# Two feed-forward barriers replaced by separate places, and memory attention laid between its projections

## The chip, the cores and the metric

The kernel runs on one core of a Trainium2 chip: TensorE (matrix products), VectorE, ScalarE and GpSimd (elementwise work), SyncE (issues DMAs), an on-chip memory of 128 partitions (SBUF) and the accumulators that TensorE writes (PSUM, eight banks of 128 x 512 float32). The metric is the device time of one execution in microseconds, median of the runs.

## The reference

One program computes two transformer-like blocks on 512 tokens of width 1024, all in float32. Only the parts that the change touches are shown.

```python
# first block: twice (layer 0 and 1), after a Mamba-2 and a Conformer mixer
u = rms_norm(x, norm_ffn[l]) @ f_up_w[l]          # 1024 -> 2 x 2816
a, g = split(causal_conv3(u, f_conv_w[l], f_conv_b[l]))
x = x + (silu(a) * g) @ f_down_w[l]               # 2816 -> 1024
# second block, after self attention, a state space model and w_out
x = layer_norm(ALPHA * x + ..., ln1)
m = layer_norm(mem, mem_ln)                       # 256 rows
k, v = split(m @ w_xkv)                           # 1024 -> 512 and 512
q = x @ w_xq                                      # 4 heads of 128
x = layer_norm(ALPHA * x + softmax(q k^T * X_SCALE) v @ w_xo, ln2)
x = layer_norm(ALPHA * x + moe_ffn(x), ln3)       # router, 64 experts, shared expert
```

## The kernel before

Activations lie transposed: features on the partitions, 512 tokens along the free side, a tensor of 1024 features being 8 blocks of 128 x 512. Each engine has one program in a fixed order; they meet through semaphores (`wait_ge`, `then_inc`).

**Rounded products.** Most projections take their precision from three products of rounded numbers (float32r): weight and activation are each split into a rounded part ("hi") and the remainder ("lo"), and TensorE does hi x hi, hi x lo and lo x hi per block of 128 (`proj_split`, L1246). ScalarE makes the hi parts (`split_half`, L1943; `split_x`, L1960), VectorE subtracts to get the lo parts (L2556, L2569). A few projections, among them memory keys, queries, values and output, use plain float32 products instead (`tile`, L1205); the profile counts two matmul instructions for each of these.

**Weights.** SyncE loads them into a ring of two slots (`wring`) in three DMAs each (L673). `slot()` waits until the tiles that used the slot before are done:

```python
if state["slots"] >= NSLOT:
    sp.wait_ge(tile_done, tiles.v - state["last"])
```

For the down projection `loop(4, 2, 2, body2)` sets `state["last"]` to 1, so the first down slot is issued when 43 of the 44 up tiles are done. The lo part is written over the slot; the hi parts lie in `whi` (at the end of the arena) for up weights and in `wdhi` (over `uT` and `sq`, which hold the up projection's input) for down weights.

**Feed-forward.** The up projection has 11 slots of 4 tiles (5 loop turns of 2 slots, and one more), 44 tiles of 8 blocks, a pair of tiles giving one block of the gated product: VectorE scales each tile out of PSUM (L2633), convolves it (L2635, L2637), ScalarE does Silu (L2162), VectorE multiplies (L2848) into `ffa`, 22 blocks. Then comes a barrier of all engines (`phase_end`: drain, count, wait for the three others), since `ffhi`, the rounded `ffa`, and the hi weights take memory that the up projection uses. After it `split_both` rounds the first half of the first down weights, 11 blocks, the second half, 11 blocks, and TensorE runs 8 down tiles of 22 blocks.

**Memory attention.** PE's order: key projection (4 tiles, 8 blocks, 256 columns), statistics of the layer norm, value projection (2 tiles), query projection (4 tiles), 16 items (4 heads by 4 groups of 128 tokens), output projection (8 tiles of 4 blocks). An item is: scores (TensorE, L1684), copy out of PSUM (VectorE, L3147), maximum (L3148), its negative (L3149), exponential with sum (ScalarE, L2341), reciprocal and product (VectorE, L3154, L3156), two transposes (TensorE, L1691), copy (ScalarE, L2349), product with the values (TensorE, L1699). PE works on scores of item n, transposes of n - 2 and values of n - 3 in one step. VectorE copies each head's result (L3160, L3162). Key, query and output weights are used as they were loaded.

**After it** come residual, layer norm, router, shared expert and then 64 experts, whose weights are loaded by L926 and L933; the first of these loads waits for the root of the last norm (`sp.wait_ge(std_ready, NORMS)`).

Of the kernel before, what the change touches and what calls it, by code (L numbers as in the profile page):

```python
# [32 lines left out]
P = 128  # L33
T = 512
# [115 lines left out]
def build(nc, A, out):  # L150

    ctx = ExitStack()
    with ctx:
# [163 lines left out]
        sgate = [carve(T) for _ in range(2)]  # L317
        ffhi = carve_r(FFN_TILES, T)
        ffhi_end = top[0]
# [74 lines left out]
        top[0] = NBANK * T + (2 * FFN_TILES + 2) * T  # L394
        assert top[0] >= ffhi_end
# [3 lines left out]
        bim = carve(S5T, 16)  # L399
        el = carve(STEPS, S5T)  # L400
        phs = carve(STEPS, S5T)
        phc = carve(STEPS, S5T)
        phr = std[:, 0:STEPS * S5T].rearrange("p (m j) -> p m j", j=S5T)
# [45 lines left out]
        memc = carve(NK, 256)  # L449
        top[0] = GATE_TOP  # L450
        memq = carve(NK, 256)
# [8 lines left out]
        vx = carve(2, T)  # L460
        top[0] = NBANK * T
        ox = carve(4, T)
# [189 lines left out]

        def phase_end(eng, me, ph):

            ph.inc()
            eng.drain().then_inc(done[me], 1)
            for other in done:
                if other != me:
                    eng.wait_ge(done[other], ph.v)


        @block.sync
        def _(sp):
# [232 lines left out]
            for e in done:  # L896
                sp.wait_ge(done[e], 6)
# [82 lines left out]
            with sp.If(crowded > CAP):  # L980
                for e in done:
                    sp.wait_ge(done[e], 7)
# [4 lines left out]
                for e in done:  # L987
                    sp.wait_ge(done[e], 8)
# [31 lines left out]
        def _(pool):  # L1020
# [22 lines left out]
            for _ in range(4):  # L1043
                phase_end(pool, "pool", ph)
# [134 lines left out]
        def _(pe):  # L1179
# [252 lines left out]
            def ffn():  # L1432
# [11 lines left out]
                phase_end(pe, "pe", ph)  # L1444

                with pe.Fori(0, 2) as i:
                    tiles.enter(i, 4)
                    slots.enter(i, 4)
                    nw.enter(i, 8)
                    for q in range(4):  # L1450
                        proj_split(FFN_TILES, ffhi, ff_lo, wdhi, range(1), fresh=q == 0)
                tiles.leave(2)
                slots.leave(2)
                nw.leave(2)
                nx.inc(FFN_TILES)

            ffn()
# [37 lines left out]
            ffn()  # L1495
# [180 lines left out]
            def attention(s, n_items, per_head, blocks, q, k, v, o, probs, turned, before):  # L1676

                for n in range(n_items + 3):
                    if n < n_items:
                        before(n)  # L1680
                        if n >= 2:
                            pe.wait_ge(s["masked"], n - 1)
                        nb = blocks(n)
                        nc.tensor.matmul(mp[n % 2][:, 0:nb * P], q(n), k(n, nb), start=True, stop=True).then_inc(s["scores"], 1)  # L1684
                    m = n - 2
                    if 0 <= m < n_items:
# [3 lines left out]
                        for j in range(blocks(m)):  # L1690
                            ins = nc.tensor.transpose(mp[2][:, j * P:(j + 1) * P], probs[m % 3][:, j * P:(j + 1) * P], ident[:])  # L1691
                        ins.then_inc(s["turned"], 1)
                    m = n - 3
                    if 0 <= m < n_items:
                        pe.wait_ge(s["evac"], m + 1)
                        if m % per_head == 0 and m:
                            pe.wait_ge(s["out"], m // per_head)
                        for j in range(blocks(m)):
                            ins = nc.tensor.matmul(o(m), v(m, j), turned[m % 2][:, j * P:(j + 1) * P],  # L1699
                                                   start=j == 0, stop=j == blocks(m) - 1)  # L1700
                        ins.then_inc(s["pv"], 1)

# [30 lines left out]
            w = slot_wait()[:, :].rearrange("p (k n) -> p k n", n=512)  # L1733
            for m in range(4):
                tile([(w[:, k, m * P:(m + 1) * P], mT[:, k, :]) for k in range(NK)], n=256)
# [7 lines left out]
            proj(NK, hT, 4)  # L1743
            q_tiles = tiles.s - 4

            def query_taken(n):
                if n % TC == 0:
                    pe.wait_ge(tile_evac, q_tiles + n // TC + 1)

            attention(att[1], 16, 4, lambda n: 2,  # L1750
                      lambda n: qx[:, n // TC, (n % TC) * P:(n % TC + 1) * P],
                      lambda n, nb: kx[:, n // TC, :],
                      lambda n, j: vx[:, j, (n // TC) * P:(n // TC + 1) * P],
                      lambda n: mp[3][:, (n % TC) * P:(n % TC + 1) * P],
                      xpb, xpt, query_taken)
            pe.wait_ge(att[1]["out"], 4)
            proj(4, ox, 8)
# [155 lines left out]
        def _(act):  # L1913
# [240 lines left out]
            def ffn(each=None):  # L2154
# [11 lines left out]
                with act.Fori(0, 5) as i:  # L2166
# [5 lines left out]
                tiles.leave(5), nconv.leave(5), nsilu.leave(5), nglu.leave(5), slots.leave(5)  # L2172
# [12 lines left out]
            ffn()  # L2185
# [51 lines left out]
            ffn(state_exponentials)  # L2237
# [98 lines left out]
            def attention(s, n_items, blocks, scale, probs, turned, nmx, rsm, after):  # L2336
# [1233 lines left out]
```

## Time and profile before

| | us |
|---|---|
| median of 3 runs (lowest, highest) | 2917.62 (2913.74, 2921.96) |
| the profiled execution | 2924.28 |
| its span, first to last instruction | 2922.5 |
| busy: TensorE / VectorE / ScalarE / GpSimd | 2710.5 / 1989.0 / 1381.3 / 230.7 |
| mean granted TensorE clock | 0.967 of full |

The span is what the profile covers; the execution's own time lies 1.8 us above it. A busy TensorE includes queued instructions: the duration of a matmul (about 0.4 us) is longer than the distance between two. So a rate is read from the length of an unbroken stretch of the chain divided by its matmuls.

### The profile page before, as it was taken

The page shows a single profiled execution, that of the slowest core. Times are in us where ns is not written, and L with a number is a line of the kernel's source. Part 1 is how long each engine was busy: PE and PEld are TensorE (multiplying, and loading weights), DVE is VectorE, ACT ScalarE, POOL GpSimd, SP SyncE. Part 2 cuts the span into 40 slices and gives each one's busy share as a digit, 9 for nine tenths or more (in the row PEclk, how much of TensorE's full clock was granted, in tenths as well). Part 3 has the DMA queues.
Part 4 walks back from the last instruction along what each step waited for, and adds up shares of the span by engine and source line. Part 5 has one row for each costly group of instructions (what it writes and reads, how often), then busy time and mean ns, then how long its engine had stood idle before and what let it go on. Part 6 is the DMA issues. An engine that isn't in the chain of part 4 may idle for free.

```text
span 2922.5 us, 36040 instructions
## 1 busy us (share of the span) xinstructions
PE 2710.5 (93%) x12225; PEld 2050.5 (70%) x12225; DVE 1989.0 (68%) x3048; ACT 1381.3 (47%) x2121; POOL 230.7 (8%) x207
## 2 busy tenths in 40 slices
PE   7999899999897989999899988999799999999996
PEld 6777778788786867888776755675357777777773
DVE  4677645677626975777538555454549999999986
ACT  4666543222324545222324333433338777777772
POOL 0000000000000000000004400000012222222210
PEclk9999999999999999999999998999899999999998
DMA  3222312232232101231633550323149999999996
GB/s 104 65 65 58 93 60 87 87 104 97 60 99 86 58 29 58 87 112 60 103 97 117 135 104 17 126 83 112 59 164 363 342 339 345 348 338 343 338 348 266
DMA packets 317001, 435.00 MB, mean 149 GB/s; under 512 B 45275, under 2 KB 198947, under 8 KB 316643
## 3 DMA queue, kind: packets, MB, share of 16 engines
q1 hardware_dynamic: 299139, 395.61, 41.8%
q0 software_dynamic: 17760, 38.06, 4.3%
q8 instruction: 60, 0.98, 0.1%
q14 instruction: 42, 0.34, 0.0%
HBM read 416.33 MB, written 42.43 MB: 157 GB/s over the span
## 4 chain that ended last, share of the span: by engine, by line
PE 64%; SPq 19%; DVE 8%; ACT 4%; issue 3%; DMA 2%; DVEq 0%; ACTq 0%; POOLq 0%
PE tp L1246 42%; SPq L926 12%; SPq L933 7%; PE tp L1205 5%; PE tp L1299 2%; PE tp L1301 2%; PE tp L1300 2%; DMA sq<-ytab 1%; PE mp L1474 1%; PE mp L1473 1%; PE mp L1475 1%; PE mp L1666 1%; PE mp L1265 1%; PE mp L1646 1%; DMA uT<-in_w_exp_gu 1%
## 5 line engine op out<-in xcount | busy, mean ns | idle before, releaser
L1246 PE MATMUL tp<-sq_r,arena_r 128*128 128x512 f32 x1152 | 464.3, 403 | 38.6 <-DVE uT_r L2569 25.7
L1246 PE MATMUL tp<-sq_r,wring_r 128*128 128x512 f32 x1152 | 459.4, 399 | 0.0
L1246 PE MATMUL tp<-uT_r,arena_r 128*128 128x512 f32 x1152 | 457.0, 397 | 0.0
L1246 PEld LDWEIGHTS tp<-sq_r,arena_r 128*128 128x128 f32 x1152 | 218.3, 190 | 98.8 <-issue 45.0
L1246 PEld LDWEIGHTS tp<-uT_r,arena_r 128*128 128x128 f32 x1152 | 218.7, 190 | 54.2 <-issue 1.9
L1246 PEld LDWEIGHTS tp<-sq_r,wring_r 128*128 128x128 f32 x1152 | 218.4, 190 | 53.6
L1246 PE MATMUL tp<-arena_r,wring_r 128*128 128x512 f32 x608 | 241.6, 397 | 0.0
L2556 DVE TENSOR_TENSOR wring_r<-wring,arena_r 128x2048 fp32r<-128x2048 f32 x80 | 182.5, 2322 | 61.8 <-ACT arena_r L1943 61.8
L2162 ACT ACTIVATE arena<-arena 128x512 f32<-128x512 f32 x44 | 27.8, 632 | 292.6 <-DVE arena L2637 292.5
L1943 ACT ACTIVATE arena_r<-wring 128x2048 fp32r<-128x2048 f32 x80 | 148.6, 1905 | 34.1 <-DMA wring<-in_a_out_proj 10.9
L1246 PE MATMUL tp<-arena_r,uT_r 128*128 128x512 f32 x480 | 152.7, 400 | 7.7 <-DVE arena_r L2569 7.7
L1246 PE MATMUL tp<-arena_r,sq_r 128*128 128x512 f32 x480 | 152.2, 398 | 7.7 <-DVE arena_r L2569 7.7
L1930 ACT ACTIVATE raw<-tp 128x512 f32<-128x512 f32 x74 | 43.7, 598 | 233.5 <-PE tp L1246 175.8
L3422 DVE TENSOR_TENSOR arena_r<-arena,arena_r 128x1024 fp32r<-128x1024 f32 x128 | 150.4, 1216 | 0.5 <-ACT arena_r L2470 0.5
L2637 DVE SCALAR_TENSOR_TENSOR arena<-raw,pcol,arena 128x512 f32<-128x512 f32 x176 | 132.3, 752 | 24.4 <-DVE arena L2637 6.1
L1299 PE MATMUL tp<-sq_r,wring_r 128*128 128x512 f32 x320 | 133.8, 418 | 8.7 <-issue 8.7
L1246 PEld LDWEIGHTS tp<-arena_r,wring_r 128*128 128x128 f32 x608 | 115.5, 190 | 27.1
L1301 PE MATMUL tp<-sq_r,wring_r 128*128 128x512 f32 x320 | 129.5, 405 | 0.0
L1300 PE MATMUL tp<-uT_r,wring_r 128*128 128x512 f32 x320 | 129.4, 405 | 0.0
L2470 ACT ACTIVATE arena_r<-arena 128x1024 fp32r<-128x1024 f32 x128 | 127.8, 1050 | 0.0
L1138 POOL DMA_INDIRECT ytab<-arena x64 | 90.2, 1409 | 467.4 <-ACT arena L2487 467.4
L2633 DVE TENSOR_TENSOR raw<-tp,rinv 128x512 f32<-128x512 f32 x88 | 60.5, 687 | 83.6 <-PE tp L1246 83.3
(531 smaller groups left out, 5923.6 us busy)
## 6 DMA issues: line engine op xcount, KB each, us to landing
arena<-in_w_exp_down SPq DMA_DIRECT2D x64, 1024.0 KB, 17.8
wring<-in_w_exp_gu SPq DMA_DIRECT2D x64, 768.0 KB, 9.8
uT<-in_w_exp_gu SPq DMA_DIRECT2D x32, 768.0 KB, 9.9
sq<-in_w_exp_gu SPq DMA_DIRECT2D x32, 768.0 KB, 10.4
wring<-in_f_up_w SPq DMA_DIRECT2D x22, 1024.0 KB, 5.2
wring<-in_f_up_w SPq DMA_DIRECT2D x44, 512.0 KB, 6.7
wring<-in_w_exp_gu SPq DMA_DIRECT2D x32, 512.0 KB, 16.8
wring<-in_f_down_w SPq DMA_DIRECT2D x32, 448.0 KB, 5.8
```

The costliest lines, as they stand in the source:

```text
L926: sp.dma_start(dst[:, a:z, :], gu[:, a:z, :]).then_inc(wg_ready[b], 16)
L933: sp.dma_start(wdn[b].rearrange("p (k n) -> p k n", n=D), dn).then_inc(wd_ready[b], 16)
L1205: ins = nc.tensor.matmul(b[lo:hi, 0:n], w, x, start=k == 0, stop=k == len(mms) - 1)
L1246: ins = nc.tensor.matmul(b[:], parts[wp][:, kk, m * P:(m + 1) * P], xparts[xp][:, kk, :], start=n_k == 0 and q == 0, stop=n_k == k - 1 and ...
L1299: nc.tensor.matmul(bank[:], w_hi[:, kk, cs], u_hi[1][:, kk, :], start=kk == 0, stop=False)
L1300: nc.tensor.matmul(bank[:], w_hi[:, kk, cs], u_lo[1][:, kk, :], start=False, stop=False)
L1301: ins = nc.tensor.matmul(bank[:], w_lo[:, kk, cs], u_hi[1][:, kk, :], start=False, stop=kk == NK - 1)
L1943: nc.scalar.activation(hi[r][1][:, a:b], wring[r][:, a:b], ACT.Copy).then_inc(whi_ready, 1)
L2470: nc.scalar.activation(wdn_hi[b][:, s], wdn[q][:, s], ACT.Copy).then_inc(moe["dhi"], 1)
L2556: V.tensor_tensor(wlo[r][:, a:b], wring[r][:, a:b], hi[r][1][:, a:b].bitcast(F32), ALU.subtract).then_inc(wlo_ready, 1)
L2637: ins = V.scalar_tensor_tensor(dst, r[:, PAD - t:PAD - t + T], w(taps - 1 - t), dst, ALU.mult, ALU.add)
L3422: V.tensor_tensor(wdn_lo[q][:, s], wdn[q][:, s], wdn_hi[b][:, s].bitcast(F32), ALU.subtract).then_inc(moe["dlo"], 1)
```

## The change

- `ffhi` moves to the end of the arena, the hi part of the first down slot's "early" weights gets a place of its own (`first_whi`). `FFN_EARLY` names the blocks whose place is free before the up projection ends: 0 to 13 in layer 0, 0 to 5 and 14 to 18 in layer 1; the others are "late".
- The barrier goes. ScalarE and VectorE round the first 9 early blocks between the last pairs of the up projection, then the first slot's early weights, the other early blocks, the last pair, the late weights and the late blocks. TensorE runs the first down tile in that order of blocks (`first_down`), and the down loop is written out.
- GpSimd takes part in two barriers instead of four; its loads for the state space model follow the Conformer's barriers. Waits on the barrier counts are renumbered.
- The key projection becomes a rounded one (`key_hi`, `mT_hi`, `mT_lo`), the output projection too (`ox_hi`, `ox_lo`).
- Query tiles 2 and 3 and 12 of the 32 blocks of the output projection stand between the steps of the attention. The maximum and the exponential read the scores from PSUM, without the copy. Heads 0 and 2 are summed in banks of the ring of tiles.

```diff
@@ places
+        FFN_EARLY = (list(range(14)), list(range(6)) + list(range(14, 19)))
+        FFN_LATE = [[k for k in range(FFN_TILES) if k not in ks] for ks in FFN_EARLY]
+        first_whi = carve_r(max(len(ks) for ks in FFN_EARLY), P)
+        top[0] = ARENA - FFN_TILES * T
         ffhi = carve_r(FFN_TILES, T)
...
+        key_hi = [None, carve_r(SLOT)]
+        ox_hi = carve_r(4, T)[1]
@@ TensorE
+            def first_down(layer):
+                early = len(FFN_EARLY[layer])
...
+                for n_k, kk in enumerate(FFN_EARLY[layer] + FFN_LATE[layer]):
+                    if n_k in (0, early):
+                        pe.wait_ge(wlo_ready, nw.v + 1)
+                        nw.inc()
+                    pe.wait_ge(xlo_ready, nx.s + n_k + 1)
+                    high = first_whi[1][:, n_k, :] if n_k < early else whole[:, kk, :]
+                    nc.tensor.matmul(b[:], high, ffhi[1][:, kk, :], start=n_k == 0, stop=False)
+                    nc.tensor.matmul(b[:], high, ff_lo[1][:, kk, :], start=False, stop=False)
+                    ins = nc.tensor.matmul(b[:], low[:, kk, :], ffhi[1][:, kk, :], start=False, stop=n_k == FFN_TILES - 1)
...
-                phase_end(pe, "pe", ph)
-                with pe.Fori(0, 2) as i:
...
+                first_down(layer)
+                for m in range(1, NK):
+                    proj_split(FFN_TILES, ffhi, ff_lo, wdhi, range(1))
...
+            QUERY_STEPS = [(0, 1), (2, 3), (4, 5), (6, 7), (0, 1), (2, 3), (4,), (5,), (6, 7)]
+            OUT_STEPS = {9: ((0, 0),), 10: ((1, 0),), 11: ((2, 0),), 12: ((0, 1),), 13: ((1, 1),), 14: ((2, 1),), 15: ((0, 2),),
+                         16: ((1, 2), (2, 2)), 17: ((3, 0), (3, 1)), 18: ((3, 2),)}
+            def memory_attention(n_weights, n_rows):
+                for n in range(16 + 3):
+                    if n < 16:
...
+                        if n >= 2:
+                            pe.wait_ge(s["exped"], n - 1)
+                        nc.tensor.matmul(mp[n % 2][:, 0:256], qx[:, h, c * P:(c + 1) * P], kx[:, h, :], start=True, stop=True)
...
+                    if n < 9:
+                        query_piece(2 + n // 4 if n < 7 else 3, QUERY_STEPS[n])
+                    for m, k in OUT_STEPS.get(n, ()):
+                        out_piece(m, k, n_weights, n_rows)
@@ ScalarE
-                for p in range(2):
-                    pair(p)
-                phase_end(act, "act", ph)
-                split_both(wdhi, FFN_TILES, P, ff_lo, ffhi)
+                pair(0)
+                split_weight(whi, NK, 512)
+                down_hi(early[0:2])
+                pair(1)
+                down_hi(early[2:4])
+                pair(2)
+                split_weight(whi, NK, 512)
+                down_hi(early[4:6])
+                pair(3)
+                act.wait_ge(tile_done, first_tile + 40)
+                down_hi(early[6:9])
+                pair(0)
+                r = slot_in()
+                first_weights(r, early, lambda a, b: first_whi[1][...])
+                down_hi(early[9:])
+                pair(1)
+                act.wait_ge(tile_done, first_tile + 44)
+                first_weights(r, late, lambda a, b: wdhi[r][1][:, a * P:b * P])
+                down_hi(late)
...
+            take(qx[:, 0, :])
+            split_weight(wdhi, 4, 1024)
+            take(qx[:, 1, :])
...
+                if n in (4, 9):
+                    take(qx[:, 2 + n // 9, :])
+                if n in (7, 11, 15):
+                    take_heads(n // 4 - 1)
@@ VectorE
-                phase_end(dve, "dve", ph)
-                split_both(wdhi, FFN_TILES, P, ff_lo, ffhi)
+                pair(16, 0)
+                split_weight(whi, NK, 512)
+                split_x(ff_lo, ffhi, early[0:2])
+                pair(17, 1)
+                split_x(ff_lo, ffhi, early[2:4])
+                pair(18, 2)
+                split_weight(whi, NK, 512)
+                split_x(ff_lo, ffhi, early[4:6])
+                pair(19, 3)
+                split_x(ff_lo, ffhi, early[6:9])
+                pair(20, 0)
+                first_weights(r, early, lambda a, b: first_whi[1][...])
+                split_x(ff_lo, ffhi, early[9:])
+                pair(21, 1)
+                first_weights(r, late, lambda a, b: wdhi[r][1][:, a * P:b * P])
+                split_x(ff_lo, ffhi, late)
...
-                            link(V.tensor_copy(p[:, 0:nb * P], bank[:, 0:nb * P]))
-                        link(V.tensor_reduce(mx[:, n:n + 1], p[:, 0:nb * P], AX.X, ALU.max))
+                    link(V.tensor_reduce(xsm[0][:, n:n + 1], mp[n % 2][:, 0:256], AX.X, ALU.max))
...
+                if n in (7, 11, 15):
+                    low_heads(n // 4 - 1)
```

## Rows read from the trace of the kernel before

**Rows 1.** The page's part 4: the chain that ended last, shares by engine.
```profile
PE 64%; SPq 19%; DVE 8%; ACT 4%; issue 3%; DMA 2%; DVEq 0%; ACTq 0%; POOLq 0%
```

**Rows 2.** Windows, us: busy by engine (instructions), granted clock, DMA share, GB/s.
```profile
2400.00:2600.00 200.00, 187.99 (x930) 145.66 (x931) 182.68 (x282) 151.06 (x224) 43.78 (x38) 0.99 0.99 344
```

**Rows 3.** Waits of SyncE's queue from 2100 us on: total, times, longest.
```profile
SPq L926 <- ACT std L1987: 13.0, 1, 13.0
```

**Rows 4.** The whole chain in order of time: start us, us, what.
```profile
517.93 246.41 PE tp L1246 x1056
...
772.03 124.80 PE tp L1246 x528
...
1405.25 125.55 PE tp L1246 x528
```

**Rows 5.** The same chain, 755 to 800 us, piece by piece.
```profile
764.37 0.70 DVE raw L2633
...
767.32 0.69 DVE arena L2848
...
768.15 1.39 ACT sq_r L1943
...
769.66 1.62 DVE wring_r L2556
```

**Rows 6.** Windows of 1 us around the start of the down projection.
```profile
769.00:770.00 1.00, 0.00 (x0) 0.00 (x0) 0.34 (x1) 1.00 (x3) 0.00 (x0) 0.62 1.21 289
...
776.00:777.00 1.00, 1.00 (x6) 0.82 (x5) 1.00 (x3) 1.00 (x3) 0.00 (x0) 0.97 0.00 0
```

**Rows 7.** Windows: key projection, query projection, memory attention, output projection.
```profile
1971.94:1985.75 13.81, 13.81 (x66) 12.16 (x65) 9.66 (x15) 5.89 (x11) 0.00 (x0) 1.00 0.37 133
2001.04:2028.69 27.65, 27.65 (x66) 12.34 (x65) 0.00 (x0) 2.39 (x4) 0.00 (x0) 1.00 0.28 88
2028.69:2066.62 37.93, 26.55 (x128) 19.41 (x127) 24.83 (x84) 16.01 (x50) 0.00 (x0) 0.82 0.17 56
2066.62:2094.40 27.78, 27.78 (x65) 12.46 (x66) 9.00 (x13) 4.18 (x7) 0.00 (x0) 1.00 0.00 0
```

**Rows 8.** Timeline of SyncE's queue, 755 to 775 us.
```profile
758.89 7.84 SPq L673 DMA_DIRECT2D wring<-in_f_down_w  x6
```

**Rows 9.** Instructions on the weight slots, 755 to 775 us: landing.
```profile
DMA to landing us min/median/max: 4.1/5.1/5.9
```

**Rows 10.** Timelines of ScalarE and VectorE: start, us, line, operation, count.
```profile
729.05 3.71 ACT L1943 ACTIVATE arena_r<-wring 128x2048 fp32r<-128x2048 f32 x2
...
734.78 4.49 DVE L2556 TENSOR_TENSOR wring_r<-wring,arena_r 128x2048 fp32r<-128x2048 f32 x2
...
769.43 5.82 ACT L1960 ACTIVATE arena_r<-arena 128x512 fp32r<-128x512 f32 x11
...
771.20 6.70 DVE L2569 TENSOR_TENSOR arena_r<-arena,arena_r 128x512 fp32r<-128x512 f32 x11
```

**Rows 11.** Timeline of TensorE's weight loads in the expert stage.
```profile
2302.78 0.53 PEld L1796 LDWEIGHTS mp<-arena_r 128*128 128x128 f32 x4
```

**Rows 12.** Timeline of VectorE during w_out; in brackets the idle time before.
```profile
1964.50 0.69 DVE L2652 SCALAR_TENSOR_TENSOR hT<-hT,raw 128x512 f32<-128x512 f32 x1 [4.16 <-ACT raw L1930]
```

**Rows 13.** The chain inside the memory attention, 2028 to 2067 us.
```profile
2032.82 0.60 ACT arena L2341 x2
...
2049.19 0.45 PE mp L1699 x4
2049.63 0.45 PE mp L1684 x2
...
2050.56 0.43 DVE arena L3148
...
2062.69 0.22 PE mp L1691 x2
```

**Rows 14.** DMA issues, 2001 to 2003 us: line, KB each, us to landing.
```profile
wring<-in_w_xo SPq DMA_DIRECT2D x1, 1024.0 KB, 8.4
```

More of the change, by code:

```diff
@@ L651, in build, with runs @@
         s5_yev = ssd["ea"]
+        def runs(ks):
+            starts = [k for k in ks if k - 1 not in ks]
+            return [(a, next(b for b in range(a + 1, FFN_TILES + 1) if b not in ks)) for a in starts]
         def phase_end(eng, me, ph):
@@ L987, in _ @@
                 for e in done:
[L988 removed]
+                    sp.wait_ge(done[e], 6)
                 load_rest()
@@ L1674, in mixed_heads, with query_piece @@
                         chunk_results(*Y_AT[n])
[L1676 to L1680, printed above, removed]
+            def query_piece(m, ks):
+                if ks[0] == 0:
+                    pe.wait_ge(tile_evac, QUERY_TILE + m - NBANK + 1)
+                w = wring[1][:, :].rearrange("p (k n) -> p k n", n=512)
+                for k in ks:
+                    ins = nc.tensor.matmul(tp[(QUERY_TILE + m) % NBANK][:], w[:, k, m * P:(m + 1) * P], hT[:, k, :],
+                                           start=k == 0, stop=k == NK - 1)
+                if ks[-1] == NK - 1:
+                    ins.then_inc(tile_done, 1)
@@ L1742, in _ @@
             pe.wait_ge(h_ready, 3 * NK)
[L1743 to L1757, printed above, removed]
+            slot_wait()
+            assert tiles.s == QUERY_TILE
+            for m in range(2):
+                query_piece(m, range(NK))
+            slots.inc()
+            memory_attention(nw.v, nx.v)
+            for m in range(4):
+                out_piece(m, 3, nw.v, nx.v)
+            for m in range(4, 8):
+                for k in range(4):
+                    out_piece(m, k, nw.v, nx.v)
+            tiles.inc(12)
+            nw.inc(2)
+            nx.inc(4)
             sum_rows(hT, 2, OUT_CONVS)
@@ L2152, in _, with ffn, down_hi, first_weights @@
             root(0, D, 0)
-            def ffn(each=None):
+            def ffn(layer, each=None):
+                products, first_tile = 2 + nglu.s, tiles.s
+                early, late = FFN_EARLY[layer], FFN_LATE[layer]
+                def down_hi(ks):
+                    for kk in ks:
+                        act.wait_ge(glu_ready, products + kk + 1)
+                        split_x(ff_lo, ffhi, (kk,))
+                def first_weights(r, ks, spot):
+                    for a, b in runs(ks):
+                        ins = nc.scalar.activation(spot(a, b), wring[r][:, a * P:b * P], ACT.Copy)
+                    ins.then_inc(whi_ready, 1)
                 def pair(p):
@@ L2848, in pair, with first_weights @@
                     V.tensor_tensor(at(ffa, p), sgate[b % 2][:], acc[(2 * b + 1) % NBANK][:], ALU.mult).then_inc(glu_ready, 1)
-                with dve.Fori(0, 5) as i:
+                early, late = FFN_EARLY[layer], FFN_LATE[layer]
+                def first_weights(r, ks, spot):
+                    dve.wait_ge(whi_ready, nw.v + 1)
+                    for a, b in runs(ks):
+                        ins = V.tensor_tensor(wlo[r][:, a * P:b * P], wring[r][:, a * P:b * P], spot(a, b).bitcast(F32), ALU.subtract)
+                    ins.then_inc(wlo_ready, 1)
+                    nw.inc()
+                with dve.Fori(0, 4) as i:
                     tiles.enter(i, 8), nconv.enter(i, 8), nsilu.enter(i, 4), chain.enter(i, 16), nglu.enter(i, 4)
```

216 lines of the change are left out of this document (126 added, 90 removed).

## The prediction

> **What bounds the kernel now.** I read the profile in this order. First the chain that ended last, by engine [rows 1]: TensorE holds 64% of it and the weight DMAs of the experts another 19%. So up to about 2190 us a gap on TensorE is time, and after that the DMA of expert weights is. Two rows [rows 2, 3] say how the two join: the DMA engines are 99% busy between 2400 and 2600, and SyncE's loads for the experts wait for a norm root that ends the TensorE part. What TensorE saves earlier therefore starts the expert stage earlier by the same amount and is not given back.
>
> Then the places where the chain leaves TensorE. In the first feed-forward the up projection ends at 764.34 (517.93 + 246.41) and the down projection starts at 772.03 [rows 4]: 7.7 us of nothing. The chain inside it [rows 5] is strictly serial: the last up tile is read and convolved (764.37 to 767.3), gated (0.69), then the barrier opens, ScalarE rounds half the first weights (1.39), VectorE takes the remainder (1.62) and one activation block, and TensorE begins. The granted clock falls to half inside the gap and is full again only about 4 us after the restart [rows 6]. By the up projection's 246.41 / 1056 = 0.2333 us a matmul, 528 down matmuls need 123.2; they took 124.8 and 125.55 in the two layers [rows 4], so the clock costs another 1.6 and 2.3. Each barrier costs 9.3 to 10 us today, both together 19.3.
>
> The memory attention is the other hole [rows 7]: query projection 27.65, attention 37.93 with TensorE busy 26.55 of it (queued instructions and low clock included, granted clock 0.82), output projection 27.78. Sum 93.36.
>
> **Feed-forward barriers: what comes instead.** The barrier goes, but the load of the first down weights is not touched: SyncE issues it at 758.89, when tile 43 of 44 is done, 5.5 us before the up projection ends [rows 8], and a part takes up to 5.9 us to land [rows 9]. The third part is issued about 0.6 us after the first and more, so the slot is full at about 765.4, 1.0 after TensorE runs dry. Before, the barrier covered that. Now it is first in the new chain, and what is queued behind it matters: VectorE has "first weights" in its program ahead of the last pair (tiles 42 and 43), so it stands still from about 757 and does not read tiles 42 and 43 until the weights are through. ScalarE has the last pair's Silu behind its own copy too.
>
> Layer 0, in order. Rounding 14 blocks, 1792 columns, at 3.71 / 4096 us a column [rows 10]: 1.65, to 767.05. Remainder on VectorE at 4.49 / 4096: 2.0, to 769.1. TensorE restarts at 769.25, 2.8 earlier than now, still after a gap of 4.9 us in which I expect the clock to fall. VectorE goes on with 5 activation blocks at 0.61 (6.70 / 11, [rows 10]) to 772.15; the last pair, 2 x 2.86 (764.37 to 767.32, less hops) + 0.69 + hops = 6.5 [rows 5], to 778.65; the late 8 weight blocks 1.15, to 779.8; the first late activation block 0.61, so TensorE's late part begins at 780.6. TensorE has 14 x 0.70 = 9.8 us of early blocks, done at 779.05 or, with half clock, about 781. Eight late blocks take 5.6: the first down tile ends at about 786.4. Now it ends at 772.03 + 15.4 + 1.6 = 789.0. Gain 2.6. The clock loss hides in the wait for the late part, so it costs almost nothing, and the earlier restart gains little.
>
> Layer 1 rounds 11 blocks early, in two pieces. Weights 1398.6, rounding 1.5, remainder 1.7, restart 1402.0; 2 activation blocks to 1403.1; last pair to 1409.6; 11 late weight blocks 1.7, first activation block, late part at 1412.05, 11 x 0.70 = 7.7, end 1419.75, against 1405.25 + 15.4 + 2.3 = 1422.95. Gain 3.2. Both layers: 5.8.
>
> At nothing I set: the activation blocks rounded during the up projection (9 per layer, 0.53 on ScalarE and 0.61 on VectorE each). They start behind pair 16; VectorE needs 2.86 x 2 + 0.69 = 6.4 us a pair against 11.2 us of TensorE, plus 4.5 for weights in every second one [rows 10]. The last up weights are then ready at about 738.7, while TensorE asks for them at 742; without that cover of 3 us each block would cost 0.61. Also at nothing: the second down tile's weights (VectorE free at 784.7, + 1.6 = 786.3, just in time; a slip costs at most about 1 us), GpSimd's small loads (now some 300 us earlier, where nothing waits), and the unrolled loops.
>
> Bounds for this part: 0 if the new chain is as long as the old one, 19.3 if the hole closes wholly.
>
> **Key projection.** 32 k-blocks of float32 with 256 columns (13.81 us, [rows 7]) become 96 rounded ones. No row has a rounded matmul of 256 columns. From one side half of the 512-column 0.2333 is 0.117; from the other, four 128-column weight loads with almost no data took 0.53, 0.13 each [rows 11]. I take 0.126: 12.1 us, a gain of 1.7. The far bound is 0.2333 as for 512 columns: 22.4 us, a loss of 8.6. The new roundings (8 blocks of 256 and a whole weight slot: some 7 us on ScalarE, 8 on VectorE) fall on w_out's tiles 3 to 6, where VectorE sits idle 4.2 us of each 5.6 [rows 12] and ScalarE has less to do than it, and so cost nothing; without that cover they would cost their 8 us.
> The Trainium skill, "TensorE: Matmul & The Clock Gate", section "LDWEIGHTS (loading the stationary operand)", gives columns / 1.2 in ns, 107 ns for 128 columns, whatever the rows. By that rule a rounded block would not be held by its weight load, 96 would take about 11.2 by half the 512-column figure, and this term would be 2.6; the row's 0.13 is above it, so I stay by the row.
>
> **Memory attention.** The output projection turns from 32 float32 blocks (27.78 / 32 = 0.87) into 32 of three rounded matmuls (3 x 0.2333 = 0.70): 22.4, 5.4 less. An item of attention costs TensorE, at full clock, scores 0.45, two transposes 0.22, values 0.45 [rows 13]: 1.12, 17.9 for 16. TensorE's work is then 27.65 + 17.9 + 22.4 = 67.95. Two query tiles go ahead (13.8); the other two (16 blocks) and 12 output blocks are laid between the items; 20 blocks follow (14.0). A step has 1.12 + 1.73 = 2.85 us up to step 8 and 1.82 after. The loop between the engines: score 0.45, maximum 0.43 straight from PSUM (the copy of 0.43 goes), sign 0.17, exponential 0.60, copy of the turned block 0.38, with hops 2.1 [rows 13]: it fits into 2.85 and just into 1.82 + 0.45. Waits that I find by following every step: the output weights are issued at 2001.24 and the last part lands 8.4 us later [rows 14], so rounding (3.7) and remainder (4.5) run until about 2017 and the first maximum is 1.8 late: 1.1 at the third item. Output block (0, 2) in step 15 needs head 2, which ScalarE and VectorE round only behind their own step 15: 0.43 + 0.17 + 0.60 + 0.38 + 0.60 + 0.70 and hops, less TensorE's 0.7: 2.5. Smaller ones of that kind (steps 12 and 13, and the last head): 2.1. Sum 5.7, total 73.6, gain 19.8. Bounds: no wait at all 25.4; a full extra microsecond in each of 19 steps, under 1.
>
> Sum: 5.8 + 1.7 + 19.8 = 27.3. The profiled execution took 2924.28 (span 2922.5), so it would be 2897; it lies 6.7 above the median of 2917.62, from which I forecast **2890.3**.
>
> **Rivals.** A, the hole closes wholly: a gain of 19.3 instead of 5.8, 2876.8. For it: the first gated blocks and VectorE's time are there. Against: [rows 8, 9]; nothing can be rounded before 765. Chance 0.06.
> B, the interleaved attention is held by hops and the heads' rounding more than I count, 0.4 to 0.9 us in each of 19 steps: gain 10 to 20 in all, 2898 to 2908. The step's slack is only 0.1 to 0.2 from step 9 on. Chance 0.12.
> C, slower: items don't overlap. One item end to end is 0.45 + 0.43 + 0.17 + 0.60 + 0.18 + 0.37 + 0.22 + 0.38 + 0.45 with nine hops, about 4. If TensorE's order makes each step wait for the item of the step, 19 x 4 = 76 + 13.8 + 14 = 104, 10.5 more than now; with the other two terms 3 us slower, and beyond the bound at 4.3 us a step, 2927. Decides from 3.9 us a step. Today a step takes 37.93 / 16 = 2.4. Chance 0.01.
> D, it does little: the rounded key projection costs its upper bound and B comes on top, within 9 us of now. Chance 0.03.
> My forecast, gain 20 to 34: 0.78 (its own range 2883 to 2898).
>
> **How the numbers follow.** 0.3% is 8.8 us, about what a measurement of this kernel can tell from no change. Faster: A, B and mine, 0.96; same 0.03; slower 0.01. The range has A at one end and most of B at the other: 2877 to 2903.
>
> **What would show it.** After: TensorE idle 4 to 5 us, not 7.7, between up and down, ended by the first weights' remainder; VectorE idle about 10 us before that; a second pause of 1 to 2 us some 10 us into the first down tile. From the first query matmul to the last output matmul 72 to 76 us, full clock throughout, longest wait about 2.5 us in step 15. Key projection 12 us. Wrong if the slot lands earlier or the first weights don't wait for it, if VectorE doesn't finish the last up weights by 742, or if a 256-column rounded matmul costs above 0.15.

## The result and the profile after

The changed kernel takes 2891.3 us (median of 4 runs, 2887.08 to 2899.33), the kernel before 2918.25 (4 runs, 2913.74 to 2921.96). The ratio is 0.9912, 95% interval 0.9886 to 0.9937. That is 27.0 us faster; the forecast was 2890.3, a gain of 27.3. The profiled execution took 2899.33 (span 2897.6, mean granted clock 0.973 where before had 0.967).

In after's lines, L1263 is the rounded projection (before L1246), L1463 to L1465 the first down tile, L1712 a query block, L1727 to L1729 an output block, L2243 (ScalarE) and L2975 (VectorE) the first down weights, L3432 the remainder of a head.

The chain by engine is within a point what it was [rows 1]: TensorE, then the experts' DMAs.

```profile
PE 64%; SPq 19%; DVE 7%; ACT 3%; issue 3%; DMA 2%; DVEq 0%; ACTq 0%
```

**The feed-forwards.** The chain of after in order of time, the lines that answer to [rows 4]:

```profile
518.97 246.40 PE tp L1263 x1056
765.37 5.65 issue
...
789.31 107.30 PE tp L1263 x462
1151.28 246.63 PE tp L1263 x1056
1397.91 5.25 issue
...
1421.16 107.30 PE tp L1263 x462
```

The up projection is undisturbed (246.40 for 246.41), so the roundings put between its last pairs cost nothing. The hole is shorter, not closed: 5.65 and 5.25 us in place of 7.7. To compare both kernels without the border between two tiles, take the time from the end of up to the end of all eight down tiles. After: 789.31 + 107.30 - 765.37 = 131.24 and 1421.16 + 107.30 - 1397.91 = 130.55. Before: 772.03 + 124.80 - 764.34 = 132.49 and 133.24 in the same way. Gain 1.25 + 2.69 = 3.9 us.

What holds the hole open, in the timelines of ScalarE and VectorE (start, us, operation; in brackets the idle time before and what ended it):

```profile
767.16 1.70 ACT L2243 ACTIVATE arena_r<-wring 128x1792 fp32r<-128x1792 f32 x1 [14.55 <-DMA wring<-in_f_down_w]
```

```profile
768.89 2.02 DVE L2975 TENSOR_TENSOR wring_r<-wring,arena_r 128x1792 fp32r<-128x1792 f32 x1 [11.04 <-ACT arena_r L2243]
...
773.84 0.68 DVE L2753 TENSOR_TENSOR raw<-tp,rinv 128x512 f32<-128x512 f32 x1
...
780.15 1.22 DVE L2975 TENSOR_TENSOR wring_r<-wring,sq_r 128x1024 fp32r<-128x1024 f32 x1
781.29 1.89 DVE L2689 TENSOR_TENSOR arena_r<-arena,arena_r 128x512 fp32r<-128x512 f32 x3
```

ScalarE stands 14.55 us and VectorE 11.04 for a transfer that lands 1.79 us after TensorE has run dry (767.16 against 765.37). Behind it on VectorE stands the last pair, which begins at 773.84 though its tiles have been there since 765.37. Windows of 1 us (busy by engine, then the granted clock) show the other cost:

```profile
770.00:771.00 1.00, 0.00 (x0) 0.02 (x1) 1.00 (x2) 1.00 (x3) 0.00 (x0) 0.64 1.19 302
...
774.00:775.00 1.00, 1.00 (x4) 0.71 (x4) 0.96 (x2) 0.00 (x0) 0.00 (x0) 0.50 0.00 0
...
777.00:778.00 1.00, 1.00 (x5) 0.78 (x5) 0.93 (x3) 1.00 (x2) 0.00 (x0) 0.95 0.00 0
```

TensorE restarts at 771.01 at half clock (1.2 of 2.4 GHz) and has the full one only at about 777.1, 6.1 us later; before, it had it some 4 us after the restart [rows 6]. By the windows the low clock lasted the same 6.8 us in both traces (769.2 to 776.1 before, 770.3 to 777.1 after); before, 2.8 us of it fell into the gap, where it costs nothing, and after only 0.7.

**Key projection and memory attention.** Windows of after: key projection, two query tiles, attention with the other two and 12 output blocks between its steps, 20 output blocks. They answer to [rows 7].

```profile
1965.30:1976.76 11.46, 11.46 (x98) 11.31 (x96) 9.66 (x15) 5.78 (x11) 0.00 (x0) 1.00 0.46 169
1992.21:2005.94 13.73, 13.73 (x34) 6.08 (x32) 2.65 (x2) 4.90 (x4) 0.00 (x0) 1.00 0.56 177
2005.94:2051.50 45.56, 42.40 (x198) 29.75 (x196) 20.38 (x69) 18.57 (x56) 0.00 (x0) 0.96 0.15 47
2051.50:2065.70 14.20, 14.20 (x61) 11.48 (x62) 8.82 (x13) 4.20 (x7) 0.00 (x0) 1.00 0.01 2
```

Key projection 13.81 to 11.46. From the first query matmul to the last output matmul 93.36 to 73.5 (13.73 + 45.56 + 14.20). TensorE is busy 93% of the middle window where before it was 70%. Its waits in the whole stretch (total, times, longest), and the longest of them:

```profile
PE tp L1727 <- DVE arena_r L3432: 3.1, 3, 2.1
```

```profile
2042.97 0.47 PE L1727 MATMUL tp<-arena_r,uT_r 128*128 128x512 f32 x1 [2.11 <-DVE arena_r L3432]
```

Sum of the parts: 3.9 + 2.35 + 19.9 = 26.1 us, the spans differ by 24.9 and the medians by 27.0. That these agree so well is partly luck: two long stretches outside the parts differ by some 4 us each, in opposite directions. From the end of the second down to the key projection the trace before took 441.1 us and after 436.8; from the last output matmul to the end they took 828.1 and 831.9. The first difference lies in the state space part (chain of before 1704.84 to 1843.15, of after 1702.49 to 1836.92: 138.3 and 134.4). It follows the execution and not the change: mem_only, with the feed-forwards of before, takes 134.6 there, and warm_gap, with those of the change, 136.8.

### The profile page after: what moved, and what is told of

Same layout as the page of the kernel before. It is cut to its first block, busy times and chain, and to the rows that moved or that the text cites. A ratio compares the mean times of both kernels' runs of the same rounds, so it can differ in the third digit from the quotient of the medians.

```text
span 2897.6 us, 35998 instructions
## 1 busy us (share of the span) xinstructions
PE 2689.7 (93%) x12289; PEld 2048.6 (71%) x12289; DVE 1994.0 (69%) x3046; ACT 1389.5 (48%) x2137; POOL 230.2 (8%) x207
## 4 chain that ended last, share of the span: by engine, by line
PE 64%; SPq 19%; DVE 7%; ACT 3%; issue 3%; DMA 2%; DVEq 0%; ACTq 0%
PE tp L1263 41%; SPq L943 12%; SPq L950 7%; PE tp L1222 4%; PE tp L1316 1%; PE tp L1317 1%; PE tp L1318 1%; PE tp L1712 1%; DMA sq<-ytab 1%; PE mp L1504 1%; PE mp L1503 1%; PE mp L1505 1%; PE mp L1282 1%; PE mp L1696 1%; PE mp L1676 1%
## 5 line engine op out<-in xcount | busy, mean ns | idle before, releaser
L1263 PE MATMUL tp<-sq_r,arena_r 128*128 128x512 f32 x1152 | 463.6, 402 | 38.7 <-DVE uT_r L2689 25.3
L1263 PE MATMUL tp<-sq_r,wring_r 128*128 128x512 f32 x1152 | 459.3, 399 | 0.0
L1263 PE MATMUL tp<-uT_r,arena_r 128*128 128x512 f32 x1152 | 457.9, 398 | 0.0
L1263 PEld LDWEIGHTS tp<-sq_r,arena_r 128*128 128x128 f32 x1152 | 218.5, 190 | 99.7 <-issue 45.1
L1263 PEld LDWEIGHTS tp<-uT_r,arena_r 128*128 128x128 f32 x1152 | 218.7, 190 | 54.5 <-issue 1.9
L1263 PEld LDWEIGHTS tp<-sq_r,wring_r 128*128 128x128 f32 x1152 | 218.4, 190 | 53.1
L1263 PE MATMUL tp<-arena_r,wring_r 128*128 128x512 f32 x564 | 222.7, 395 | 0.0
L1263 PE MATMUL tp<-arena_r,sq_r 128*128 128x512 f32 x436 | 136.9, 396 | 0.0
L1263 PE MATMUL tp<-arena_r,uT_r 128*128 128x512 f32 x436 | 136.8, 395 | 0.0
L1263 PEld LDWEIGHTS tp<-arena_r,wring_r 128*128 128x128 f32 x564 | 106.3, 188 | 25.2
## 6 DMA issues: line engine op xcount, KB each, us to landing
sq<-in_w_exp_gu SPq DMA_DIRECT2D x32, 768.0 KB, 10.3
```

Of the source, the lines that this page charges most:

```text
L1263: ins = nc.tensor.matmul(b[:], parts[wp][:, kk, m * P:(m + 1) * P], xparts[xp][:, kk, :], start=n_k == 0 and q == 0, stop=n_k == k - 1 and ...
```

## Experiments

All times "query to output" below are from the first query matmul to the end of the last output matmul. "Down" is the time from the end of up to the end of the eight down tiles, both layers added: 265.7 before, 261.8 after. Seven versions ran once: heads_early 2887.62, warm_gap 2895.21, no_interleave 2897.55, copy_back 2899.23, copy_back_plain 2897.38, one_bank 2902.18, copy_one_plain 2907.36. Such a time can't tell a few microseconds (the kernel before took 2910.58 to 2928.17 in 13 runs, and copy_back_plain comes out below no_interleave, though its stretch is 4.75 us longer), so their verdicts rest on a stretch of the trace.

### ffn_only: the feed-forward part alone

The kernel before with the feed-forward hunks of the change (`first_down`, `FFN_EARLY`, `first_whi`, no barrier); key projection and memory attention as before.

> The kernel before with the feed-forward part of the change alone (own places for the rounded rows and for the first down weights). Theory, from the two traces: the first down tile ends 23.9 us after the up projection in layer 0 and 23.3 us in layer 1, where before it took 25.2 and 25.9, so the whole is 3.9 us faster than before (ratio 0.9987), all of it in these two gaps. Rival: the gain of the whole change was made elsewhere and the gaps give 0 or over 10 us.

Measured: 2913.99 (12 runs) against 2918.16 (17 runs), ratio 0.9983, interval 0.9972 to 0.9994, so 5.0 us, between 1.8 and 8.2. The chain:

```profile
762.39 5.61 issue
...
785.77 107.30 PE tp L1256 x462
...
1391.36 4.91 issue
...
1413.96 106.79 PE tp L1256 x462
```

Down is 130.68 + 129.39 = 260.1. The theory holds: the part is small and lies in the two gaps.

### mem_only: key projection and memory attention alone

The kernel before with the rest of the change; the barriers of the feed-forwards stay.

> The kernel before with the memory attention and the rounded key projection alone. Theory: key projection 11.5 us where before took 13.8, query start to last output matmul 73.5 us where before took 93.4: 22.2 us faster than before (ratio 0.9924). Rival: some of the gain seen in the attention stage needs the feed-forward part, and the ratio is above 0.994.

Measured: 2895.23 (4 runs), ratio 0.992, interval 0.9902 to 0.9939: 23.3 us. Query to output 73.5 (1993.92 to 2067.38), key projection 11.31, so 11.31 / 96 = 0.118 us for a rounded matmul of 256 columns:

```profile
1967.32 11.31 PE tp L1212 x96
```

The theory holds: this part needs nothing of the other, and 5.0 + 23.3 = 28.3 is the whole (25.7 by its ratio) within the intervals.

### early_load: the first down weights issued three tiles sooner

```diff
-                def body2(i):
-                    for j in range(2):
-                        slot(1, thirds(down, FFN_TILES, (2 * i + j) * P, P))
-                loop(4, 2, 2, body2)
+                for m in range(NK):
+                    slot(1, thirds(down, FFN_TILES, m * P, P))
```

> The changed kernel with the slots of the down projection written out, so that the first of them waits for 40 finished tiles of up where the loop makes it wait for 43. Theory (what holds the hole open is the late transfer of the first down weights): it is issued some 16 us earlier, the early roundings are done before the up projection ends, the engine never stops long enough to lose its clock, and the first down tile ends some 15.5 us after the up projection in both layers (66 products of 0.233 us): 16 us faster than the change, about 2875 us. Rival (the chain of the last pair on VectorE binds): the tile ends 20 us or more after it and the gain stays under 7 us.

Measured: 2872.65 (4 runs, 2870.94 to 2873.78), ratio to before 0.9845, interval 0.9827 to 0.9864. The change stands at 0.9912 (0.9886 to 0.9937), so this is some 18.6 us faster than it, of which 261.8 - 244.6 = 17.2 lie in the two gaps. The chain:

```profile
516.25 244.06 PE tp L1261 x1056
...
775.58 107.30 PE tp L1261 x462
1138.83 244.30 PE tp L1261 x1056
...
1398.40 106.79 PE tp L1261 x462
```

The first down tile ends 775.58 - 760.31 = 15.27 us after the up projection, and 15.27 in layer 1: 66 matmuls at 0.2314, no gap and no clock lost. Timelines of SyncE, ScalarE and VectorE, one fence each:

```profile
738.15 24.02 SPq L690 DMA_DIRECT2D wring<-in_f_down_w  x6
```

```profile
747.79 1.69 ACT L2241 ACTIVATE arena_r<-wring 128x1792 fp32r<-128x1792 f32 x1
```

```profile
752.82 2.02 DVE L2973 TENSOR_TENSOR wring_r<-wring,arena_r 128x1792 fp32r<-128x1792 f32 x1
...
765.22 4.91 DVE L2687 TENSOR_TENSOR arena_r<-arena,arena_r 128x512 fp32r<-128x512 f32 x8
```

The transfer is issued at 738.15, 22 us before up ends, where the change issues it 5.5 us before. The early weights are rounded at 752.82 to 754.84, inside the up projection, VectorE reads the last pair as soon as it is there, and the late blocks begin at 765.22, 4.9 us after up, where the change has them 15.9 after. The late transfer was the cause of the hole; the rival is refuted.

### early_load_before: the same edit to the kernel before

> The kernel before with the slots of the down projection written out in the same way. Theory: before, the barrier and the roundings behind it hold TensorE, and the weights have landed by then, or nearly; so the earlier transfer gives under 1 us for each layer (ratio 0.9993 to 1.000). Rival: the late transfer is a hold of its own before too, and gives 3 us or more for each layer.

Measured: 2918.09 against 2919.03, ratio 0.999, interval 0.9974 to 1.0007. The load goes out at 740.25 instead of 758.89, up ends at 762.63, down starts at 770.32, and the chain between them has the same roundings as in [rows 5]:

```profile
766.44 1.38 ACT sq_r L1941
...
767.95 1.63 DVE wring_r L2554
```

Down is 133.15 + 132.52 = 265.7, as before to 0.1 us. So the early load is worth nothing that can be measured with the barrier, and 16 to 17 us without it (244.6 against the 260.8 that eight profiles below have on average). The barrier hid the late transfer; taking the barrier away and leaving the transfer gave a fifth to a quarter of what the two give together.

### warm_gap: useless matmuls ahead of the first down tile

```diff
+                for _ in range(6):
+                    nc.tensor.matmul(mp[3][:], ones[:], hT[:, 0, :], start=True, stop=True)
                 first_down(layer)
```

> The changed kernel with six matmuls of no use ahead of the first down tile in each layer, on operands that are there already and into a bank that is free, so that TensorE is busy in the first half of the wait for the weights. Theory (the half clock after the hole costs time of its own): the clock falls later or not at all, and the first down tile of layer 0 ends 22.3 us after the up projection, where the change took 23.9; of layer 1 0 to 0.9 us sooner. Rival: the late roundings bind, and both stay within 0.3 us of 23.9 and 23.3.

Measured: first down tile 24.04 us after up in layer 0 and 24.6 in layer 1; neither theory nor rival, though layer 0 has the rival's number and layer 1 its mechanism, a wait for the late roundings. Down is 262.7, not less than the change's 261.8. In layer 1 TensorE keeps the full clock at the restart, and then this (TensorE's timeline, and its windows with the granted clock behind the busy share):

```profile
1392.80 5.31 PE L1484 MATMUL mp<-hT,ones 128*128 128x512 f32 x12
1398.17 0.47 PE L1463 MATMUL tp<-arena_r 128*128 128x512 f32 x1
...
1407.94 0.47 PE L1463 MATMUL tp<-arena_r,uT_r 128*128 128x512 f32 x1 [1.89 <-DVE arena_r L2691]
```

```profile
1399.00:1400.00 1.00, 1.00 (x6) 1.00 0.40 94
...
1411.00:1412.00 1.00, 1.00 (x3) 0.50 0.00 0
```

The early blocks are through at about 1405.8, the late ones are not rounded before 1407.9, 15.1 us after up ended, and the clock falls after that pause, where nothing covers it. In the change the late blocks began 15.4 us after up (1413.35 - 1397.91), so there were 0.3 us to gain here. In layer 0 the restart came 6.94 us after up where the change had 5.65, since the weights landed at 765.84, 3.09 us after up (1.5 to 2.0 in the eight other profiles with this part of the change; one run can't say why). From that restart the tile took 17.1 us, in the change 18.3: the clock was at half for 3.4 us of it (771.0 to 774.4 by the windows) where in the change it was for 6.1. So in layer 0 the shorter half clock gave 1.2 us of the tile; the hole itself stays.

### heads_early: the heads of the attention rounded one step sooner

```diff
-                if n in (7, 11, 15):
-                    take_heads(n // 4 - 1)
+                if n in (6, 10, 14):
+                    take_heads((n - 6) // 4)
...
-                if n in (7, 11, 15):
-                    low_heads(n // 4 - 1)
+                if n in (6, 10, 14):
+                    low_heads((n - 6) // 4)
```

> The changed kernel with the heads taken one step earlier, alone. Theory: the heads' rounding on VectorE is the wait (2.1 us at the last step, 0.7 and 0.3 us at two others); one step of 2.2 us earlier it falls to under 0.3 us in all, the clock does not fall, and the stretch from the first query matmul to the last output matmul takes some 70 us where the change takes 73.5. Rival: the waits stay, since what the rounding waits for is no sooner done.

Measured: query to output 71.2 (1985.55 to 2056.76), full clock in all of it. TensorE's waits in the stretch:

```profile
PE mp L1755 <- ACT arena L2533: 1.4, 3, 0.6
PE tp L1727 <- DVE arena_r L3432: 1.1, 2, 0.7
```

The 2.1 us wait and the clock loss are gone; 1.4 us of new, short waits on the transposes came: in the chain a head's rounding on ScalarE (0.50) and its remainder on VectorE (0.69) now stand ahead of the next item's maximum. 2.3 us of the expected 3.5.

### both: early load and earlier heads

> The early first down weights together with the heads of the memory attention taken one step earlier (steps 6, 10 and 14 where the change has 7, 11 and 15). Theory: 16 us from the holes and some 3.5 us from the waits at the ends of the steps (2.1 us before the third item of the last steps, with the clock lost behind it), so 19 us faster than the change, about 2872 us. Rival: the heads' exponentials and copies are late for an earlier step, the waits move and give nothing, about 2875 us.

Measured: 2871.69 (4 runs, 2868.36 to 2874.59), ratio to before 0.9844, interval 0.9825 to 0.9863. It is the fastest of all, but 1.0 us from early_load is less than these runs can tell; in the trace, query to output is 71.2 in it and 73.4 in early_load. The forecast of 19 us below the change came out at 19.6.

### no_interleave: nothing between the attention's steps

```diff
-                    if n < 9:
-                        query_piece(2 + n // 4 if n < 7 else 3, QUERY_STEPS[n])
-                    for m, k in OUT_STEPS.get(n, ()):
-                        out_piece(m, k, n_weights, n_rows)
...
-            for m in range(2):
+            for m in range(4):
                 query_piece(m, range(NK))
```

and all 32 output blocks behind the attention.

> The changed kernel with all four query tiles ahead of the memory attention and all output pieces behind it, nothing between the attention's steps, with the roundings as in the change. Theory: the fillers take up waits of the attention chain, so without them the stretch from the first query matmul to the last output matmul takes some 83 us where the change takes 73.5 (before: 93.4, with full-precision instructions of the plain kind in the projections). Rival: the gain lies in the rounded projections alone, and it stays within 76 us.

Measured: 77.7, between the two. Query projection, attention, output projection:

```profile
1987.64:2015.30 27.66, 27.66 (x66) 12.35 (x65) 4.49 (x2) 6.79 (x6) 0.00 (x0) 1.00 0.28 88
2015.30:2042.95 27.65, 20.07 (x129) 15.10 (x128) 17.65 (x67) 15.94 (x53) 0.00 (x0) 1.00 0.24 77
2042.95:2065.35 22.40, 22.40 (x98) 18.18 (x98) 9.70 (x14) 4.79 (x8) 0.00 (x0) 1.00 0.00 1
```

I had missed that the steps themselves got shorter: 27.65 for the same 16 items that took 37.93 before [rows 7], at full clock where before had 0.82. The fillers are worth only 4.2 us. The next four ask where the other 10.3 come from.

### copy_back, copy_back_plain: the copy of the scores put back

In the changed kernel, and in no_interleave:

```diff
+                    if n >= 3:
+                        dve.wait_ge(s["turned"], n - 2)
+                    link(V.tensor_copy(xpb[n % 3], mp[n % 2][:, 0:256]))
-                    link(V.tensor_reduce(xsm[0][:, n:n + 1], mp[n % 2][:, 0:256], AX.X, ALU.max))
+                    link(V.tensor_reduce(xsm[0][:, n:n + 1], xpb[n % 3], AX.X, ALU.max))
...
-                    nc.scalar.activation(xpb[n % 3], mp[n % 2][:, 0:256], ACT.Exp, scale=X_SCALE, ...
+                    nc.scalar.activation(xpb[n % 3], xpb[n % 3], ACT.Exp, scale=X_SCALE, ...
```

> The changed kernel with VectorE's copy of the scores out of PSUM put back: copy, maximum of the copy, exponential in place. Theory: the loop of an item grows by the copy (0.4 us) to 2.5 us; it still fits into the steps 0 to 8 with a query block (2.85 us) and costs 0.2 to 0.4 us in each of the ten later steps, so the stretch from the first query matmul to the last output matmul takes 75.5 to 77.5 us where the change takes 73.5. Rival: the later steps cover it too, and it stays within 0.5 us of 73.5.

Measured: query to output 76.6, 3.1 us more; the theory's size holds. Its place is shown in part: TensorE's listed waits grew by 1.3 us only (transposes 1.1, scores 0.2), and the clock loss is the change's; the other 1.8 us are in no list.

> The version with nothing between the attention's steps (27.7 us for the 16 items, 7.6 us of them waits, full clock) with the copy of the scores put back. Theory: without fillers the loop sets the step, each of 16 items gets 0.4 us longer, 6.4 us in all, and the 16 items take 34 us; the longer waits also take some of the clock. Rival: less than half of it, under 31 us, since two items are under way at once.

Measured: query to output 82.5, 4.75 us more than no_interleave, 0.30 an item where the theory had 0.4, at full clock. The items take 32.4, short of the theory's 34 and over the rival's 31, and the clock loss that the theory also had did not come:

```profile
2013.80:2046.20 32.40, 21.10 (x129) 14.89 (x128) 23.89 (x83) 16.58 (x53) 0.00 (x0) 1.00 0.20 66
```

### one_bank, copy_one_plain: all heads in one accumulator

```diff
-        memory_out = [tp[QUERY_TILE % NBANK], mp[3], tp[(QUERY_TILE + 3) % NBANK], mp[3]]
+        memory_out = [mp[3]] * 4
...
-                        if c == 0 and h == 3:
-                            pe.wait_ge(xlo_ready, n_rows + 2)
+                        if c == 0 and h >= 1:
+                            pe.wait_ge(xlo_ready, n_rows + h)
```

In the changed kernel, and in copy_back_plain.

> The changed kernel with all four heads summed in the same PSUM bank, so that the first product with values of a head waits until ScalarE and VectorE have rounded the head before (in the change only head 3 waits, for head 1). Theory: two more waits of 1.5 to 2 us each, at steps 7 and 11, and some clock: the stretch from the first query matmul to the last output matmul takes 76.5 to 78.5 us where the change takes 73.5. Rival: a wait here only takes the place of the one at the output blocks (step 12 and 15), and it stays under 75 us.

Measured: query to output 80.5, 7.0 us more, above the theory's range and far from the rival. The waits of the stretch:

```profile
PE mp L1766 <- DVE arena_r L3432: 8.0, 3, 2.7
...
PE tp L1727 <- DVE arena_r L3432: 0.7, 1, 0.7
```

8.7 us of waits where the change has 3.1; the other 1.4 go with the clock (0.93 in the attention's window where the change has 0.96).

> Nothing between the attention's steps, the copy put back and one bank for all heads: the attention of the kernel before, rebuilt in the changed kernel, with the rounding of a head in the place of its copy. Theory: these two are the whole of the difference between 27.7 us (no fillers) and 37.9 us (before), so the 16 items take 37 to 41 us and the granted clock in them is below 0.9. Rival: something else in the change made up the difference, and they take under 34 us.

Measured: query to output 89.45; the 16 items 38.6 us at a clock of 0.89:

```profile
2016.30:2054.90 38.60, 24.56 (x129) 18.03 (x129) 24.17 (x83) 16.57 (x53) 0.00 (x0) 0.89 0.17 55
```

The attention of the kernel before is rebuilt, within 0.7 us of its 37.93. So the chain of versions accounts for the 19.9 us: 93.4 before; 89.45 with the output projection rounded (5.4 less, 0.7 more for the items, 0.8 of half clock behind them); 82.5 with heads in separate banks (7.0); 77.7 without the copy (4.75); 73.5 with the fillers (4.2). The price of an edit depends on its neighbours: the copy costs 3.1 with the fillers and 4.75 without.

## Why the prediction was right

- **Forecast 2890.3, measured 2891.3.** The terms 5.8, 1.7 and 19.8 came out as 3.9 (5.0 in ffn_only's timing), 2.35 and 19.9. What TensorE saves does start the experts' loads sooner: the first goes out at 2080.1 us where before had 2108.8, and 24.9 of these 28.7 us are left at the end of the span. That forecast and median lie 1.0 us apart is luck all the same: the interval of the ratio leaves a gain between 18.4 and 33.3 us.
- **The hole: shortened, not closed.** "First weights" waited for the transfer and VectorE stood still about 11 us, as forecast; TensorE's gap was 5.65 and 5.25 us where the forecast had 4 to 5. Rival A (19.3 us) did not come, for the reason given [rows 8, 9], and early_load shows that this reason is the only one: with the transfer out of the way down falls by 265.7 - 244.6 = 21.1, more than A's 19.3.
- **The term that was mis-sized: 5.8 us for both layers.** The pair of traces gives 3.9. Eight profiles of kernels with this part of the change as it stands (after, ffn_only, heads_early, no_interleave, copy_back, copy_back_plain, one_bank, copy_one_plain) have down between 259.9 and 261.8, mean 260.8; three without it (before, mem_only, early_load_before) 265.7, 266.7, 265.7, mean 266.0. That is 5.2, so of the 1.9 us that the pair of traces lacks 1.3 are variation between executions. Within the pair, two steps came out longer. The slot landed 1.8 and 2.0 us after up, not 1.0, and TensorE restarted 0.7 and 0.8 us later than forecast. And the step "The clock loss hides in the wait for the late part" failed: in layer 0 the half clock lasted 6.1 us after the restart where I had counted on the 4 us of before, the early part (done at 783.8) was then later than the first late block (ready at 781.9), nothing was left to hide in, and the tile took 18.3 us from the restart where I had 17.15 (layer 1: 18.0 for 17.75). Against that I had the first tile of before 1.1 us too short for both layers together (24.66 and 25.39 after up, against 25.19 and 25.94). My 786.4 is also a slip: 780.6 and eight blocks of 0.70 give 786.2. The second pause that I expected inside the first tile is absent since TensorE never caught up with VectorE; warm_gap, where TensorE kept the full clock through the early part of layer 1, brought it back there (1.89 us).
- **The key projection**: 0.118 us a matmul. I had taken 0.126, between 0.117 and 0.13. The rule of the Trainium skill ("TensorE: Matmul & The Clock Gate", section "LDWEIGHTS (loading the stationary operand)", 107 ns for 128 columns), by which the weight load would not hold a matmul of this size, was nearer than my row [rows 11]: it gave 2.6, the chain has 13.81 - 11.31 = 2.5.
- **The attention**: 73.6 forecast, 73.5 measured, but two errors cancel. I counted 5.7 us of waits, there were 3.1: none at the third item (the first maximum was 1.3 us late where I had 1.8, and its exponential was through at 2008.9, before TensorE came to the third scores at 2010.24), 2.1 of the 2.5 in step 15, 1.0 of the 2.1 small ones. Against that the clock, which I had at full throughout, fell behind the wait in step 15 (about 1.7 us lost by the windows below), and 0.7 us more are in no list of waits: 73.5 - 67.95 - 3.1 - 1.7. One_bank and copy_back cost 7.0 and 3.1 us, together about half of the gain. The prediction names the missing copy in its count of a step. The separate banks it does not name: that no head but one waits for the rounding of another is in its count unsaid, so it had the right sum without the part that was worth most.

## What to carry to other kernels

When a barrier is taken away, ask what it was covering: here a weight transfer that a loop's coarse wait (43 tiles where 40 are enough) let out too late. Neither edit alone was worth more than about 5 us of 2918, both together 21. And a useful cross-check of a forecast is to rebuild the old version inside the new one, one edit at a time: the interleaving, which looks like the point of the change, gave 4.2 of 19.9 us, while an accumulator bank of its own for every other head gave 7.0 (each price holds for this order of edits).

## What the runs showed that I had not expected

- **The clock falls in a busy stretch.** After the 2.11 us wait of step 15, TensorE's windows (busy, granted clock):

```profile
2042.00:2043.00 1.00, 0.03 (x1) 1.00 0.00 0
...
2044.00:2045.00 1.00, 1.00 (x6) 0.50 0.00 0
...
2047.00:2048.00 1.00, 1.00 (x10) 1.00 0.00 0
```

  About 3.4 us at half clock (0.72 in the window from 2043, 0.57 in that from 2046), with TensorE at work on both sides. In warm_gap the clock fell behind a wait of 1.89 us in the same way. Not every wait of this length does it: in copy_back_plain two of 1.80 us, and in one_bank the third of three waits of 2.67, left the clock at full; behind the two others of one_bank it fell. No run here says what decides.
- **How long the half clock lasts differs between executions of the same code**: in the first feed-forward it ran until 6.1 us after the restart in after and only until about 2.8 in no_interleave (769.57 to 772.4; the window from 772 has 0.82, the next 1.00). Counted from its fall, the low clock lasted 6.8 us in the one and 3.4 in the other, and 10.2 in the second feed-forward of before (1400.7 to 1410.9), behind the same 7.7 us gap as in the first, where it was 6.8. The first down tile ended 18.3 and 16.9 us after the restart accordingly.

```profile
772.00:773.00 1.00, 1.00 (x5) 0.79 (x4) 1.00 (x2) 0.00 (x0) 0.00 (x0) 0.82 0.00 0
```

  The second feed-forward of before (busy, granted clock):

```profile
1400.00:1401.00 1.00, 0.00 (x0) 0.85 1.13 341
...
1410.00:1411.00 1.00, 1.00 (x4) 0.53 0.04 8
```

- **Two steady rates at a granted clock of 1.00.** The same 1056 matmuls of the up projection take 246.4 us (0.2333 each) in some executions and 244.05 (0.2311) in others, and both can occur in one execution: 246.40 in layer 0 and 244.30 in layer 1 of the run called both, and likewise in mem_only and no_interleave. No run here says why; it makes 2.3 us a phase of noise, as much as some edits above.
